# Choosing on chip which three experts close an MoE stage, with 128 slots each, in a hybrid decoder step

## The reference, cut to what matters

```python
def hier_moe(h, prm):                     # h: T x 1024
    pg = softmax(h @ w_route_group + b_route_group)       # 4 groups
    g_idx = argmax(pg)                                    # one group per token
    le = (h @ w_route_expert + b_route_expert).reshape(T, 4, 4)
    le_g = le[token, g_idx]                               # the 4 experts of that group
    top_p, top_i = top_k(softmax(le_g), 2)                # two of them
    wts = g_w * top_p / sum(top_p)
    e_idx = g_idx * 4 + top_i
    ...
    y[t] += wts * ((silu(x @ w_gate[e]) * (x @ w_up[e])) @ w_down[e])   # FF = 512
x = x + hier_moe(rmsnorm(x))
y = rmsnorm_final(x)
```

## Time and profile before

| what | value |
|---|---|
| median of 3 runs | 1231.43 us (1229.28 to 1262.04) |
| the profiled execution | 1221.8 us, its span 1220.0 us |
| PE busy | 1131.7 us, 93% of the span |
| PEld, DVE, ACT, POOL busy | 794.6, 467.5, 365.1, 268.5 us |
| chain that ended last | PE 85%, DVE 9%, issue 2%, ACT 2% |
| HBM | 148.30 MB read, 28.41 MB written |

### The profile page before, as it was taken

One profiled execution on the slowest core, in us unless ns is written; L12 is line 12 of the kernel. 1 busy time (PEld: TensorE's weight loads), 2 busy tenths in 40 slices (PEclk: granted clock), 3 DMA queues, 4 the chain that ended last, 5 costly groups with the idle time before them and its releaser, 6 DMA issues.

```text
span 1220.0 us, 25056 instructions
## 1 busy us (share of the span) xinstructions
PE 1131.7 (93%) x10930; PEld 794.6 (65%) x10930; DVE 467.5 (38%) x937; ACT 365.1 (30%) x817; POOL 268.5 (22%) x163
## 2 busy tenths in 40 slices
PE   6999999999999878777789999899999999999995
PEld 4666666655566666757554444387788887887883
DVE  4200656356765676676625422530011110001143
ACT  3101546344334365553521311111101111111152
POOL 0000000001110189999500000112112111111103
PEclk9999989999999999999999999989999999999998
DMA  6511100010100300002241751278889979999963
GB/s 207 146 35 39 53 18 18 18 35 22 39 25 15 65 6 4 4 3 55 45 154 21 254 210 61 89 274 285 291 290 311 307 266 323 340 320 345 374 259 113
DMA packets 96410, 175.00 MB, mean 143 GB/s; under 512 B 20394, under 2 KB 41709, under 8 KB 95892
## 3 DMA queue, kind: packets, MB, share of 16 engines
q1 hardware_dynamic: 88708, 152.11, 35.9%
q0 software_dynamic: 7584, 21.20, 6.7%
HBM read 148.30 MB, written 28.41 MB: 145 GB/s over the span
## 4 chain that ended last, share of the span: by engine, by line
PE 85%; DVE 9%; issue 2%; ACT 2%; SPq 0%; DMA 0%; POOLq 0%; POOL 0%; DVEq 0%
PE ps L756 22%; PE ps L1457 21%; PE ps L1256 9%; PE ps L1482 9%; PE ps L1488 2%; PE ps L835 1%; PE ps L859 1%; PE ps L848 1%; PE ps L1432 1%; PE ps L972 1%; DVE ps L2322 1%; PE ps L960 1%; PE ps L1013 1%; DVE arena L2311 1%; PE ps L1002 1%
## 5 line engine op out<-in xcount | busy, mean ns | idle before, releaser
L756 PE MATMUL ps<-arena 128*128 128x355 f32 x960 | 302.5, 472 | 1.9 <-issue 1.8
L1457 PEld LDWEIGHTS ps<-arena 128*128 128x128 f32 x2048 | 254.6, 191 | 7.5 <-issue 6.5
L1457 PE MATMUL ps<-arena 128*128 128x160 f32 (+4 forms) x2048 | 257.3, 288 | 0.6 <-ACT arena L1987 0.6
L756 PEld LDWEIGHTS ps<-arena 128*128 128x128 f32 x960 | 182.0, 193 | 109.2 <-issue 13.5
L1256 PE MATMUL ps<-arena 128*128 128x512 f32 x256 | 116.5, 597 | 0.7 <-DVE arena L2385 0.7
L1482 PE MATMUL ps<-arena 128*128 128x512 f32 x256 | 113.5, 595 | 0.8 <-DVE arena L2660 0.8
L1995 ACT ACTIVATE arena<-ps 128x160 f32<-128x160 f32 (+4 forms) x64 | 18.7, 291 | 288.3 <-PE ps L1457 288.3
L2660 DVE TENSOR_TENSOR arena<-arena,ps 128x160 f32<-128x160 f32 (+4 forms) x64 | 19.5, 305 | 222.7 <-ACT arena L1995 222.7
L2853 POOL TENSOR_TENSOR arena<-arena 128x1024 f32<-128x1024 f32 x4 | 11.4, 2854 | 334.4 <-DVE arena L2186 334.4
L1482 PEld LDWEIGHTS ps<-arena 128*128 128x128 f32 x256 | 47.2, 190 | 54.3 <-issue 53.0
L1584 ACT COPY arena<-ps 128x355 f32<-128x355 f32 x60 | 27.2, 453 | 184.5 <-PE ps L756 184.5
(11 more groups left out here) (422 smaller groups left out, 1560.6 us busy)
## 6 DMA issues: line engine op xcount, KB each, us to landing
arena<-in_w_exp_gate SPq DMA_DIRECT2D x16, 2048.0 KB, 11.0
arena<-in_w_exp_up SPq DMA_DIRECT2D x16, 2048.0 KB, 17.0
arena<-in_w_exp_down SPq DMA_DIRECT2D x16, 2048.0 KB, 15.8
arena<-in_w_in SPq DMA_DIRECT2D x16, 512.0 KB, 3.9
arena<-in_x_prompt SPq DMA_DIRECT2D x9, 512.0 KB, 3.5
x_dram<-arena SPq DMA_DIRECT2D x9, 512.0 KB, 3.6
h_dram<-arena SPq DMA_DIRECT2D x8, 512.0 KB, 2.6
out_y_prompt<-arena SPq DMA_DIRECT2D x8, 512.0 KB, 3.2
```

The costliest lines, as they stand in the source:

```text
L756: last = pe.matmul(ps[:, q % 2, 0:m], wr[:, n % 3, k, :], hT[:, k, a:a + m], start=(k == 0), stop=(k == KB - 1))
L1457: last = pe.matmul(ps[:, 3 + f % 2, n * CAP:n * CAP + CAPS[e]], w[a][:, k, f * P:(f + 1) * P], xgT[:, a, k, 0:CAPS[e]], start=(k == 0), st ...
```

## The change

The three last experts are no longer fixed. On the counts plus `key0`, DVE takes the least of each group (expert 0 is kept out by its bonus), leaves out the group whose least is the largest, and gives the three others a key below all the rest; the ranking then works as before, and the three stand in falling order in places 13 to 15. These places have 128 slots instead of 160 and so no tail. The other twelve follow in falling order as before, but three of them are others now, and place 8 has 136 slots (with a tail) instead of 128. Everything that served the tails of the last three places goes: their transposes and down matmuls, `xsB`, `quarter_sums`, `gq`, `c_same`, their sums, roots, reciprocals, scalings and indexed stores. SP now reads the expert of places 13 to 15 from the computed order.

With the counts above the order before is 0, 10, 8, 5, 3, 9, 6, 14, 2, 1, 4, 12, 13, 7, 11, 15 and after it 0, 10, 8, 5, 3, 9, 6, 11, 14, 2, 7, 12, 15, 1, 4, 13. After, the loads by place are 145, 157, 155, 150, 139, 136, 132, 132, 129, 128, 128, 119, 114, 122, 122, 104.

```diff
-CAPS = [160, 160, 160, 152, 144, 144, 136, 136, 128, 128, 128, 128, 128, 160, 160, 160]
+CAPS = [160, 160, 160, 152, 144, 144, 136, 136, 136, 128, 128, 128, 128, 128, 128, 128]
...
-ENDS = list(range(2 * EPG - 1, NE, EPG))
...
     key = (NE - 1 - x) / NE + 4096.0 * (x == FIRST)
-    for n, k in enumerate(ENDS):
-        key[k] -= 4096.0 * (n + 1)
...
-                if p >= ACC:
-                    return ENDS[p - ACC]
...
-                    if e == 2:
-                        sp.dma_start(same, i["c_same"]).then_inc(s["x0"], 16)
...
                 turn(r, NE - 1)
-                down_ready(r, NE - 2)
-                for n in range(2):
-                    down_half(r, NE - 2, n)
-                pe.wait_ge(s["fn_act"], FA * r + 13)
-                down_tail(0)
-                gate_up(r, NE - 1, lambda f: quarter_sums(1) if f == 2 else None)
-                down_ready(r, NE - 1)
-                down_half(r, NE - 1, 0)
-                pe.wait_ge(s["fn_act"], FA * r + 17)
-                pe.wait_ge(s["yo_dve"], NOUT * (r + 1) - 2)
-                down_tail(1)
-                down_half(r, NE - 1, 1, lambda: quarter_sums(2))
+                down(r, NE - 2)
+                gate_up(r, NE - 1)
+                down(r, NE - 1)
...
                         root(10, stat[:, 0:10]).then_inc(s["fn_act"], 1)
-                        act.wait_ge(s["fn_pe"], FP * r + 1)
-                        root(30, ps[:, 7, TD:TD + 1]).then_inc(s["fn_act"], 1)
                         table(ACT.Silu, 52)
...
                     link(dve.tensor_tensor(st_["key"], X["cnt"], key0, ALU.add))
+                    by4x4 = lambda ap: ap.rearrange("p (g j) -> p g j", g=NG)
+                    link(dve.tensor_reduce(st_["least"], by4x4(st_["key"]), AX.X, ALU.min))
+                    link(dve.tensor_reduce(st_["most"], st_["least"], AX.X, ALU.max))
+                    link(dve.scalar_tensor_tensor(st_["least"], st_["least"], st_["most"], st_["least"], ALU.is_lt, ALU.mult))
+                    link(dve.tensor_tensor(by4x4(st_["above"]), by4x4(st_["key"]), st_["least"][:, :, None].to_broadcast([P, NG, EPG]), ALU.is_equal))
+                    link(dve.scalar_tensor_tensor(st_["key"], st_["above"], -4096.0, st_["key"], ALU.mult, ALU.add))
...
-                    dve.tensor_tensor(st_["cown"], st_["kown"], own0, ALU.subtract).then_inc(s["r_dve"], 1)
+                    link(dve.tensor_tensor(st_["above"], X["cnt"], mine, ALU.mult))
+                    dve.tensor_reduce(st_["cown"], st_["above"], AX.X, ALU.add).then_inc(s["r_dve"], 1)
```

More of the change, by code:

```diff
@@ L126, in constants @@
     key = (NE - 1 - x) / NE + 4096.0 * (x == FIRST)
-    for n, k in enumerate(ENDS):
-        key[k] -= 4096.0 * (n + 1)
-    place = c[None, :] - NE * (i[:, None] % (2 * NE) // NE)
+    place = np.where(c[None, :] // NE == i[:, None] % (2 * NE) // NE, np.array(RANK * 2)[None, :], -1)
     caps = np.tile(CAPS * 2, (P, 1))
-    sort = np.concatenate([place, caps, np.tile(key, (P, 1)), key[i % NE][:, None], (i % NE)[:, None], i[:, None] % NE == x], axis=1)
+    sort = np.concatenate([place, caps, np.tile(key, (P, 1)), (i % NE)[:, None], i[:, None] % NE == x], axis=1)
     assert sort.shape[1] == SORT_W
-    return {"c_sort": sort.astype(np.float32), "c_prefix": prefix.astype(np.float32), "c_same": same.astype(np.float32), "c_table": table.astype(np.float32), "c_level": level, "c_bias": bias.astype(np.float32),
+    return {"c_sort": sort.astype(np.float32), "c_prefix": prefix.astype(np.float32), "c_table": table.astype(np.float32), "c_level": level, "c_bias": bias.astype(np.float32),
             "c_sbias": sbias.astype(np.float32)}
@@ L347, in program @@
         sort = part(R0, SORT_W)
-        place, caps, key0, own0, eown, mine = (sort[:, a:b] for a, b in ((0, 32), (32, 64), (64, 80), (80, 81), (81, 82), (82, 98)))
+        place, caps, key0, eown, mine = (sort[:, a:b] for a, b in ((0, 32), (32, 64), (64, 80), (80, 81), (81, 97)))
         R0 += SORT_W
@@ L351, in program @@
         for n, k in (("stackP", 32), ("key", 16), ("above", 16), ("t32", 32), ("cp", 16), ("capE", 16), ("ct", 18),
-                     ("slotsF", CAP), ("over", 8), ("qf", 1), ("kown", 1), ("rown", 1), ("capown", 1), ("cown", 1), ("top", 1)):
+                     ("slotsF", CAP), ("over", 8), ("qf", 1), ("least", 4), ("most", 1), ("kown", 1), ("rown", 1), ("capown", 1), ("cown", 1), ("top", 1)):
             st_[n] = part(R0, k)
@@ L1533, in one_round @@
                     gate_up(r, e)
-                def quarter_sums(k):
-                    pe.wait_ge(s["fn_act"], FA * r + (1, 15, 19)[k])
-                    pe.matmul(ps[:, 7, TD:TD + 1], same, stat[:, (50, 35, 47)[k]:(51, 36, 48)[k]], start=True, stop=True).then_inc(s["fn_pe"], 1)
                 turn(r, NE - 2)
@@ L2800, in one_round @@
                     elif e:
-                        for h in range(3):
+                        for h in range(2):
                             sums(e - 1 - ACC, h)
@@ L2930, in one_round @@
                         put(x_dram, xsA[k], rowA[:, e:e + 1], TOK - 1)
-                        put(x_quarters, xsB[:, k, :], rowB[:, e:e + 1], TQ * TOK - 1)
-                    pool.wait_ge(s["fo_out"], 32 * LAST * r)
+                    pool.wait_ge(s["fo_out"], 16 * LAST * r)
                     alone(pool)
@@ L2982, in _ @@
             pool.wait_ge(s["h2o1"], H2O[1] + 16 * 4 + 16 * 4 * past)
-            for k, (outA, outB) in enumerate(((eyA[:, 1, :], eyB[:, 1, :]), (eyA[:, 0, :], eyB[:, 0, :]), (X2[:, 0, :], X2[:, 1, 0:TD]))):
+            for k, out in enumerate((eyA[:, 1, :], eyA[:, 0, :], X2[:, 0, :])):
                 e = ACC + k
-                parts = ((y_rows, ys_rows, outA, rowA[:, e:e + 1], smpA, (SEQ, NS), (1, 3, 7)[k]),
-                         (y_quarters, ys_quarters, outB, rowB[:, e:e + 1], smpB, (TQ * SEQ, TQ * NS), (2, 4, 6)[k]))
-                for prompt, sample, out, rows, smp, n, ready in (parts[::-1] if k == 2 else parts):
-                    alone(pool)
-                    pool.wait_ge(s["fn_dve"], FD * past + ready)
-                    alone(pool)
-                    put(prompt, out, rows, n[0] - 1)
-                    put(sample, out, smp[:, k:k + 1], n[1] - 1)
+                alone(pool)
+                pool.wait_ge(s["fn_dve"], FD * past + (1, 2, 4)[k])
+                alone(pool)
+                put(y_rows, out, rowA[:, e:e + 1], SEQ - 1)
+                put(ys_rows, out, smpA[:, k:k + 1], NS - 1)
 def kernel(**inputs):
```

116 lines of the change are left out of this document (40 added, 76 removed).

## The result

The changed kernel took 1210.41 us (median of 4 runs, 1207.35 to 1212.92) against 1230.36 us (median of 4, 1228.1 to 1262.04); the ratio, from fast runs alone, so without the 1262.04, is 0.984 (95% interval 0.980 to 0.988). In a second, larger measurement it took 1210.47 us (median of 6, 1208.11 to 1215.57) against 1224.27 us (median of 17, 1216.93 to 1228.62): ratio 0.991 (0.9875 to 0.994). Between executions of one kernel lie up to 12 us, which is as much as the change brings, so two small samples can give different ratios. Both changes are smaller than 2%. Over the runs of both measurements the time goes with the mean granted clock of PE; lines fitted to the 17 runs before and the 10 after give 1223.7 and 1210.8 at their common mean of 0.979. That is 12.9 us or 1.05%, against a forecast of 11.65 us or 0.95%.

What follows compares the result with a forecast made beforehand. PE's chain of waits was taken to bound the kernel from place 1 on. Terms -16.1 + 2.7 + 1.25 + 0.5 = -11.65 us (-0.95%), put on the median of 1231.43, gave 1219.7 us; range 1209 to 1227.

Steps and rivals of the forecast that it cites:

- Places 13 to 15 and place 8: PE's chain: narrower places 13 to 15 without tails save 16.1 us; place 8, widened with a tail, costs 2.7.
- One round: Loads fit their slots, so no second round; rival of some 400 us more (1630 us), chance 0.01.
- Routing: Five linked DVE steps ahead of the ranking cost 1.05 us, a sixth 0.2; 1.25 us in all (0.9 to 1.65).
- ACT in place 14: Silu and squares outlast PE's shorter slices; PE idles 0.4 us before `down(14)`, 0.5 us taken in all (0 to 1.5).
- The second half of the step: ACT's remaining squares, function tables and place 15's copies: 7.7 us against PE's 7.8 plus 0.4, fitting to within 0.1.
- The weights' queue: Place 15's up weights land 1.4 us before PE needs them, no stall; rival stall of 2 us or more, chance 0.15.
- The row of 400 GB/s: DMA rate in the trace from 1142.5 to 1152 us, which the forecast counted with for the weights' queue.
- half microsecond of stall: By the skill page's 358 GB/s, the queue's later half takes some 2 us more and place 15 waits about 0.5.
- The end: Behind the last down half the chain stays the same; POOL's fewer stores for places 13 and 14 change nothing.
- The clock as a rival: More idle PE in routing shifts its clock, costing 2 us or returning 1 to 2; chance beyond 1 us 0.1.

Runs made afterwards that it cites:

- The kernels without the search: Changed kernel, last three experts fixed on the host, five DVE steps left out: 0.988 of the kernel before; also without two PE fillers, list matmul at 6.88 us.
- the kernel with place 8 alone: Kernel before with one edit, place 8 at 136 slots and a tail instead of 128: ratio 1.001 (0.9986 to 1.0034).
- the fillers: Two 256-column PE fillers left out of the changed kernel and its twin without the five DVE search steps: list matmul at 7.78 and 6.88 us.
- the changed kernel with the copy: Changed kernel plus an unread 4.2 MB HBM-to-HBM copy in SP's queue before place 15's weights: PE stalled 9.6 us.
- the kernel before with the copy: Kernel before plus the same unread 4.2 MB HBM-to-HBM copy in SP's queue before place 15's weights: PE stalled 1.9 us.

## Why the prediction was right, point by point

**The time: the difference right, the level in part luck.** The forecast was 1219.7 us in a range of 1209 to 1227, the measured 1210.41 lies 1.4 above its low end. The terms account for 1.0 of the 9.3 us between them (-12.7 against -11.65). The rest comes from the level of the runs and from the gap of 20 us between the medians of the first measurement, which the second (13.8) did not repeat. The time is inside the range because the low end had been worked out from the faster profiled execution, 1221.8, not because of a term. The errors of the terms nearly all go one way, and nothing large cancels.

**Places 13 to 15 and place 8: right.** PE sets the pace of every place, and the price of a part can be read from another place of the same width. Measured -16.3 and +2.74 against -16.1 and +2.7; the place 8 term was confirmed alone.

**One round: right.** The chain holds one round of 16 places.

**Routing: right for DVE, about a quarter too high for PE.** DVE's masking ends 1.13 later (1.25). The forecast took PE and ACT's cover as used up, from a profile where DVE waited 0.12 for PE; at the lower clock the kernel before has 0.61 of it. And the clock behind the lists was left out of the sum. What reaches gate and up of place 0 is 15.25 to 15.84 against 14.59 to 14.89 over four profiles each, in the mean 0.9. The kernels without the search show that it isn't to be had back one for one.

**ACT in place 14: right place, size three times too high (0.5 against 0.16).** The forecast reckoned 3.77 us and 0.05 for a silu and three squares, from a silu's start to the end of the last accumulator read. ACT's timeline shows the silus now paced by ACT itself:

```profile
1161.67 0.28 ACT L1960 ACTIVATE arena<-ps 128x128 f32<-128x128 f32 x1 [2.26 <-PE ps L1440]
...
1165.22 0.19 ACT L1977 ACTIVATION_READ_ACCUMULATOR arena<-arena 128x1 f32 x1
1165.31 0.26 ACT L1960 ACTIVATE arena<-ps 128x128 f32<-128x128 f32 x1
...
1168.92 0.26 ACT L1960 ACTIVATE arena<-ps 128x128 f32<-128x128 f32 x1
```

The next silu starts before the read is over, at 3.64 and 3.61 us, only 0.04 to 0.07 above PE's slice. So nothing was lost ahead of `down(14)` by the starts of the chain (forecast 0.4). The second half of the step, tables and copies against 7.8 us of PE, came out: from 1168.92 to 1176.70, 7.78 us (forecast 7.7), with 0.16 of waiting where 0.1 stood.

**The weights' queue: no stall, as taken;** the margin was 3.0 instead of 1.4, for the queue was 1.7 us shorter than taken, and not through place 8. SP asked for `X2` 3.2 us ahead of place 15's weights (1144.23 against 1147.45), where the forecast had about 2. The row of 400 GB/s held after, too: 1148 to 1155 moved at 411 and 1170 to 1176 at 400 to 408, and there the queue was still full:

```profile
1148.00:1155.00 7.00, 7.00 (x23) 3.41 (x21) 1.14 (x2) 0.22 (x1) 0.97 (x1) 1.00 1.02 411
...
1173.00:1176.00 3.00, 3.00 (x8) 1.33 (x7) 1.64 (x3) 2.96 (x5) 0.00 (x0) 1.00 1.03 408
```

The 358 GB/s that the Trainium skill, DMA: Bandwidth & Descriptors, "Where 436 GB/s comes from", gives as binding was not a ceiling for this core in these stretches, so its half microsecond of stall did not come. That estimate was a little high as well: the trace before has 381 GB/s over the later half (1142.5 to 1167.7), by which that figure would make it 1.6 us longer, and the wait 0.2.

**The end: 0.3 better than nothing, through no term.** POOL's last pair of stores began 1.20 us behind the end of DVE's last scaling before (1210.76 to 1211.96) and 0.88 after (1202.13 to 1203.01). The tails' stores are not the reason: before, POOL was through with them at 1210.2, and in the kernel with place 8 alone, which has them all (the last ends at 1210.83), it is 0.88 as well (1211.38 to 1212.26). The other two profiles of the kernel before have 1.21. The cause is open, and the 0.3 can't be put down to the change.

**The clock as a rival.** It moved single executions by far more than the 1 or 2 us that the forecast gave it, only not through the change: the first one-hot product comes between 784.4 and 793.4 us, and that lies ahead of the routing. Behind it, gate and up of place 0 stayed at 17.62; from the first list matmul to its start pass 7.5 to 8.5 us, by the clock of that stretch.

## What to carry to other kernels

Where one engine carries the whole chain, price a change of width from another row of that engine, and expect each term to be right to a few tenths; the error sits in the engines that had cover before, so read their period from start to start, not to the end of their last record. When slots shrink, look again at everything that was hidden under them: here ACT's squares and the weights' queue went from 0.7 us a slice and 12 us of room to nothing and 3. When an edit seems to move a point, look whether the difference is already there ahead of it, as with the fillers. And when runs of one kernel scatter as widely as the change is large, measure from a marker in code that the change doesn't touch.

## What the runs showed of the hardware

The same code up to the routing took between 784.4 and 793.4 us in twelve profiles; in the stretch shown first the granted clock was at 0.86 of full speed in one and at 1.00 in the other, in the same part of the code. And a stall can cost more than itself: after the 9.6 us that PE stood in the changed kernel with the copy, gate and up of place 15 took 16.06 us, where the changed kernel has 14.56. PE had been idle since 1167.6; the granted clock was 0.58 in the first 4 us behind the stall, so mostly at the level of 1.2 GHz, and 1.00 in the next 4:

```profile
1177.00:1181.00 4.00, 3.87 (x21) 3.90 (x22) 0.00 (x0) 0.00 (x0) 0.00 (x0) 0.58 1.02 412
```

After a stall of 1.9 us, in the kernel before with the copy, gate and up kept its 8.93 us a half (8.96 without the copy), at a granted clock of 1.00. The Trainium skill, TensorE: Matmul & The Clock Gate, "What's actually happening", says that the throttled state is the default and activity releases it; the trace agrees: the clock was down behind the 9.6 us of idle time and came back with PE at work, at a cost of 1.5 us.
